# Order of work around the heads of a hybrid decoder layer: twelve key groups ahead of the heads with values in turns, early raw rows, forget sums ahead of a weight split

## The reference

```python
x @ w_in  ->  rq, rk (4 heads x 128, rotary), rv, rg (4 x 256), fq, fk, fv (8 heads x 64), ff, ga, gb (1024 each)
logf = log_sigmoid(ff + b_f)
# prompt: retention in chunks of 128, and forgetting attention:
logits = q k^T / 8 + cumsum(logf)_q - cumsum(logf)_k, causal; p = softmax; o = p v
# samples: retention from a state; attention over 4096 cached rows each, in 32 pages of 128 rows:
k_past = cache_k[page_table]; v_past = cache_v[page_table]; lf_past = cache_logf[page_table]
# merge, then DeepNorm and a causal convolution FFN:
u_a = (silu(rg) * group_norm(ret_o)) @ w_pa;  u_b = fox_o @ w_pb
mix = (sigmoid(ga) * u_a + sigmoid(gb) * u_b) @ w_o
h = layer_norm(2**0.25 * x + mix);  a = gelu(conv(h @ w_up)) * (h @ w_gate)
y = layer_norm(2**0.25 * h + a @ w_down)
```

## Time and profile before

| | |
|---|---|
| median of 3 runs | 2079.36 us (2076.39 to 2080.16) |
| profiled execution | 2078.71 us, of which the span of instructions is 2076.8 us |
| PE busy | 1964.2 us (95%) |
| DVE busy | 1143.8 us (55%) |
| ACT busy | 646.4 us (31%) |
| POOL busy | 195.4 us (9%) |
| mean granted clock of PE | 0.981 |

### The profile page before, as it was taken

How to read it: one execution, slowest core, us unless ns; L and a number is a source line. 1 busy time by engine, 2 the same in 40 slices (tenths; PEclk the granted TensorE clock), 3 DMA queues, 4 the chain that set the end, 5 groups by cost and what they waited for, 6 DMA issues and landing times.

```text
span 2076.8 us, 38216 instructions
## 1 busy us (share of the span) xinstructions
PE 1964.2 (95%) x14259; PEld 1839.1 (89%) x14259; DVE 1143.8 (55%) x1748; ACT 646.4 (31%) x1196; POOL 195.4 (9%) x230
## 2 busy tenths in 40 slices
PE   7999999899999999979899998999999999999996
PEld 5888888788898898868799997999999999999996
DVE  5545646968867866875423857633322333234348
ACT  5445433134134133313401304433202231133334
POOL 1000000111020020010000100000000001000005
PEclk9999999999999999999999999999999999999999
DMA  5111113697987988886833411111111111211154
GB/s 155 43 42 42 41 54 104 216 323 238 323 278 245 314 273 285 285 296 226 283 92 97 119 51 31 32 51 41 51 50 41 51 40 45 58 41 41 38 163 135
DMA packets 151730, 276.63 MB, mean 133 GB/s; under 512 B 19057, under 2 KB 57982, under 8 KB 151590
## 3 DMA queue, kind: packets, MB, share of 16 engines
q1 hardware_dynamic: 115954, 175.22, 25.4%
q0 software_dynamic: 23296, 82.96, 13.7%
q10 hardware_dynamic: 12368, 16.88, 2.2%
HBM read 247.37 MB, written 27.72 MB: 132 GB/s over the span
## 4 chain that ended last, share of the span: by engine, by line
PE 74%; DVE 12%; DMA 4%; issue 4%; SPq 3%; ACT 2%; POOL 0%; ACTq 0%; DVEq 0%; POOLq 0%
PE bank L125 55%; PE bank L142 5%; PE bank L1718 3%; PE bank L521 2%; PE bank L948 2%; DVE cache_keys L1245 2%; PE bank L533 2%; DVE score L1249 2%; SPq L836 2%; DMA cache_keys<-in_cache_k_dram 1%; SPq L828 1%; DMA cache_vals<-in_cache_v_dram 1%; PE banks L505 1%; PE banks L507 1%; DVE w_lo L108 1%
## 5 line engine op out<-in xcount | busy, mean ns | idle before, releaser
L125 PE MATMUL bank<-x_hi,w_hi 128*128 128x344 f32 x1872 | 612.0, 327 | 16.1 <-DVE rot_sin L1315 12.6
L125 PE MATMUL bank<-x_hi,w_lo 128*128 128x344 f32 x1872 | 602.8, 322 | 0.0
L125 PE MATMUL bank<-x_lo,w_hi 128*128 128x344 f32 x1872 | 602.5, 322 | 0.0
L125 PEld LDWEIGHTS bank<-x_hi,w_hi 128*128 128x128 f32 x1872 | 356.3, 190 | 30.0 <-issue 17.4
L125 PEld LDWEIGHTS bank<-x_hi,w_lo 128*128 128x128 f32 x1872 | 356.3, 190 | 0.0
L125 PEld LDWEIGHTS bank<-x_lo,w_hi 128*128 128x128 f32 x1872 | 355.9, 190 | 0.2 <-issue 0.2
L101 ACT ACTIVATE w_hi<-w_raw 128x1024 fp32r<-128x1024 f32 (+3 forms) x139 | 142.1, 1023 | 388.9 <-PE bank L125 371.3
L125 PE MATMUL bank<-moving_lo,w_hi 128*128 128x344 f32 x744 | 239.0, 321 | 0.0
L125 PE MATMUL bank<-moving_hi,w_hi 128*128 128x344 f32 x744 | 226.0, 325 | 9.2 <-DVE moving_lo L1886 3.3
L108 DVE TENSOR_TENSOR w_lo<-w_raw,w_hi 128x1024 fp32r<-128x1024 f32 (+1 forms) x138 | 164.2, 1190 | 87.4 <-ACT w_hi L101 86.8
L125 PE MATMUL bank<-moving_hi,w_lo 128*128 128x344 f32 x648 | 209.0, 323 | 0.0
(11 more groups left out here) (292 smaller groups left out, 2817.8 us busy)
## 6 DMA issues: line engine op xcount, KB each, us to landing
cache_keys<-in_cache_k_dram SPq DMA_DIRECT2D x256, 256.0 KB, 4.9
cache_vals<-in_cache_v_dram SPq DMA_DIRECT2D x256, 256.0 KB, 5.3
w_raw<-in_w_in_dram POOLq DMA_DIRECT2D x52, 512.0 KB, 6.4
w_raw<-in_w_up_dram POOLq DMA_DIRECT2D x22, 512.0 KB, 4.6
w_raw<-in_w_gate_dram POOLq DMA_DIRECT2D x22, 512.0 KB, 4.6
tail_raw<-in_w_down_dram SPq DMA_DIRECT2D x22, 448.0 KB, 3.6
gate<-gate_t_scratch SPq DMA_DIRECT2D x15, 516.0 KB, 3.5
w_raw<-in_w_down_dram POOLq DMA_DIRECT2D x10, 448.0 KB, 4.4
```

Of the source, the lines that this page charges most:

```text
L125: mm = pe.matmul(g.bank[n][0:m, 0:TC], w[slot][:, k, 0:m], x[:, k, chunk(n)], start=(k == 0 and i == 0), stop=(k == kt - 1 and i == 2))
```

## The change

**Start.** The split of the first query weights moves behind the page sums, on ACT behind the copies of the forget logits, on DVE behind the first step of the log sigmoid.

**Heads.** `KEYS_AHEAD` places 12 of sample 0's 16 key groups ahead of the heads, none among the query rotations. The other four, its maximum and shift go into the first head's value products; ACT's exp and GpSimd's maximum move there too, the latter behind the loads of weights 6 and 7. The first head has tables of its own, in which sample 1's keys start at step 4 and sample 0's values at step 6. SP's order follows: one quad of sample 0's values goes between its last two quads of keys, then a quad of sample 1's keys, and so on in turns.

**Raw rows.** Six of the eight gated rows go to a buffer of their own (`gated_early`, over the key slots and part of the bias) and are loaded in pairs right behind the last values, ahead of SP's four small stores. The last two are loaded behind the wait for all stores. ACT waits for the last cache transpose and the stored states at the end of `retain`, DVE for the stored gated rows. `HELD_AFTER` becomes (3, 4, 7).

**Attention tiles.** Two tiles are loaded when the gates' buffers are free, two after the first chunk of the last w_pa product; ACT and DVE split all four in thirds, each third after its chunk of that product.

Moved allocations, counts of semaphores that follow from this, and loops written anew without a change of order are left out below.

```diff
@@ -308,7 +308,6 @@
             round_half(QB, 0, NS, g.xh[:, :, SEQ:T])
-            split_hi(g, act, job(0, 0, 1))
@@ -316,6 +315,7 @@
                 act.activation(rows[s][:, 0:FH], later[s], ACT.Copy).then_inc(first_row, 1)
+            split_hi(g, act, job(0, 0, 1))
@@ -358,7 +358,6 @@
             split_half(QB, 0, NS, slice(SEQ, T))
-            split_lo(g, dve, job(0, 0, 1))
@@ -369,6 +368,7 @@
             ch.link(dve.scalar_tensor_tensor(zn[:], z[:], -1.0, z[:], ALU.mult, ALU.min))
+            split_lo(g, dve, job(0, 0, 1))
@@ -706,6 +706,10 @@
 KEYS_A = (1, 1, 1, 1, 1, 1) + (0, 1, 0, 1, 0, 1, 0, 1, 0) + (1, 0, 1, 0, 1, 0, 1) + (2,)
+KEYS_AHEAD = (0, 0, 2, 1, 2, 1, 0, 1, 5)
+AHEAD = sum(KEYS_AHEAD)
+VALUES_A_FIRST = (0, 0, 0, 0, 0, 0) + (1, 1, 0, 1, 1, 1, 1, 1, 1) + (1, 0, 1, 1, 0, 1, 1) + (1, 0, 1, 1)
+KEYS_A_FIRST = (0, 0, 0, 0, 1, 1) + (1, 0, 1, 1, 0, 1, 1, 0, 1) + (1, 1, 1, 0, 1, 1, 1) + (2,)
@@ -839,45 +844,67 @@
             sp.wait_ge(g.fo_stored, FH // 2 * 16)
...
+            def load_quad(ring, land, used, cache, n, q):
+                ids = page_ids(n, q)
                 for slot in range(SLOTS):
...
+                    load_group(ring, land, used, cache, n, q, slot, ids)
+            def load_both(n, q, of, quad):
+                key_ids, value_ids = page_ids(n, q), page_ids(of, quad)
+                for slot in range(SLOTS):
+                    load_group(keys, k_land, k_used, ck, n, q, slot, key_ids)
+                    load_group(vals, v_land, v_used, cv, of, quad, slot, value_ids)
+            QUADS = NG // SLOTS
+            with sp.Fori(0, QUADS - 2) as q:
+                load_quad(keys, k_land, k_used, ck, 0, q)
+            load_both(0, QUADS - 2, 0, 0)
+            load_quad(keys, k_land, k_used, ck, 0, QUADS - 1)
+            load_quad(keys, k_land, k_used, ck, 1, 0)
+            def period(n, ahead=0):
+                with sp.Fori(ahead, QUADS) as q:
+                    load_both(n + 1, q, n, q)
+            def next_q(n, u):
+                sp.wait_ge(new_mult, n + 1)
+                load_q(n + 2, u)
+            period(0, 1)
+            next_q(0, 0)
+            period(1)
+            next_q(1, 1)
+            with sp.Fori(1, RH - 1) as h:
...
-                    sp.wait_ge(new_mult, h * 2 + u + 1)
-                    load_q(h * 2 + u + 2, u)
+                    next_q(h * 2 + u, u)
             period(NS - 2)
...
+            with sp.Fori(0, QUADS) as q:
+                load_quad(vals, v_land, v_used, cv, NS - 1, q)
+            sp.wait_ge(biased, NS * 2)
+            sp.wait_ge(k_used, NS * NG + SLOTS)
+            sp.wait_ge(g_stored, (RH - 1) * 32)
+            g.load_gated_early(sp)
...
             sp.wait_ge(new_stored, 64)
-            sp.wait_ge(fos_out, NS)
-            for j in range(FH // 2):
-                sp.dma_start(g.fo_dram[j, :, SEQ:T], fos[:, j, :]).then_inc(g.fos_stored, 16)
...
             sp.wait_ge(fin_stored, RH * 16)
+            g.load_gated_late(sp)
+            sp.wait_ge(fos_out, NS)
+            for j in range(FH // 2):
+                sp.dma_start(g.fo_dram[j, :, SEQ:T], fos[:, j, :]).then_inc(g.fos_stored, 16)
@@ -892,7 +919,6 @@
                 load(0, j)
-            all_max(0)
@@ -903,6 +929,8 @@
                     load(h, j)
+                if h == 0:
+                    all_max(0)
@@ -972,7 +1000,7 @@
                 def values_a(e):
-                    for i in take(VALUES_A_LAST if last else VALUES_A, e):
+                    for i in take(VALUES_A_LAST if last else VALUES_A if h else VALUES_A_FIRST, e):
@@ -1135,7 +1163,6 @@
                 gate_chunk(J0 + 3, 3 + n, 0, 1, n, silus[2 + (3 + n) % 4])
-            cache_exp(0, 0)
@@ -1159,6 +1186,8 @@
+                        if h == 0 and w == 5 and n == 1:
+                            cache_exp(0, 0)
@@ -1233,6 +1262,8 @@
             heads(act, body)
+            act.wait_ge(turned, NS)
+            act.wait_ge(fin_stored, RH * 16)
@@ -1325,14 +1356,12 @@
                         split_lo(g, dve, job(J0, 1, 4))
-                    for i in share(NG, 9, 3 * w + n):
+                    for i in take(KEYS_AHEAD, 3 * w + n):
                         cache_logits(0, 0, i)
-            cache_max(0, 0)
-            cache_shift(0, 0)
...
                 def keys_a(e):
-                    for i in take(KEYS_A_LAST if last else KEYS_A, e):
+                    for i in take(KEYS_A_LAST if last else KEYS_A if h else KEYS_A_FIRST, e):
@@ -1347,9 +1376,18 @@
                         keys_a(3 * (w - 4) + n)
-                        if w == 4 and n == 0:
+                        if h and w == 4 and n == 0:
                             cache_sum(h * 2, 0)
+                        if h == 0:
+                            for i in share(NG - AHEAD, 3, n) if w == 4 else ():
+                                cache_logits(0, 0, AHEAD + i)
+                            if w == 4 and n == 2:
+                                cache_max(0, 0)
+                            if w == 5 and n == 1:
+                                cache_shift(0, 0)
                 nxt(6)
+                if h == 0:
+                    cache_sum(0, 0)
@@ -1450,6 +1488,7 @@
             heads(dve, body)
+            dve.wait_ge(g_stored, RH * 32)
@@ -1474,7 +1513,10 @@
     LANDS = 4
-    HELD_AFTER = (2, 5, 7)
+    EARLY_RAW = KD - 2
+    LAND = [(0, 1), (0, 1), (1, 1), (1, 1), (2, 1), (2, 1), (3, 1), (0, 2), (1, 2), (2, 2), (3, 2), (0, 3)]
...
+    HELD_AFTER = (3, 4, 7)
@@ -1501,7 +1543,7 @@
-        fo_slot = [z[:, KB + n, :] for n in range(KB)]
+        g_early = nc.alloc_sbuf_tensor_at("gated_early", [P, EARLY_RAW, T], F32, offset=g.keys_end - EARLY_RAW * T * 4)
@@ -1513,7 +1555,10 @@
-        raw = [g_raw[:, n, :] for n in range(KD)] + [gate[0][:], gate[1][:], stage[0][:, 0:T], fo_slot[3]]
+        raw = [g_early[:, n, :] for n in range(EARLY_RAW)] + [g_raw[:, n, :] for n in range(EARLY_RAW, KD)]
+        fo_raw = [[x[:, chunk(n)] for n in range(NCH)] for x in (gate[1], stage[0])] + [
+            [g_raw[:, at + n, chunk(0)] for n in range(NCH)] for at in (KD - 2 * NCH, KD - NCH)]
@@ -1536,6 +1581,16 @@
+        def load_gated_early(sp):
+            for n in range(0, EARLY_RAW, 2):
+                sp.dma_start(g_early[:, n:n + 2, :], g.g_dram[n:n + 2].rearrange("a p t -> p a t")).then_inc(s_land[LAND[n][0]], 16)
+        def load_gated_late(sp):
+            sp.dma_start(raw[KD - 2], g.g_dram[KD - 2]).then_inc(s_land[LAND[KD - 2][0]], 16)
+            sp.wait_ge(s_hi, 2)
+            sp.dma_start(raw[KD - 1], g.g_dram[KD - 1]).then_inc(s_land[LAND[KD - 1][0]], 16)
...
@@ -1544,25 +1599,21 @@
-                sp.dma_start(raw[n], g.g_dram[n] if n < KD else g.fo_dram[n - KD]).then_inc(s_land[n % LANDS], 16)
...
...
             sp.wait_ge(g.fos_stored, 16 * (FH // 2))
-            for b in (0, 1):
-                for n in range(NCH):
-                    sp.wait_ge(g.bank_free[n], JA + KD - 1 - b + 1)
-                load_raw(KD + b)
-            load_raw(KD + 2)
-            sp.wait_ge(g.mm_chunk, NCH * (RING + JB))
-            load_raw(KD + 3)
-            for i in range(KD, 2 * KD):
-                if i < KD + 2:
-                    sp.wait_ge(s_lo, i + 1)
+            for n in range(NCH):
+                sp.wait_ge(g.bank_free[n], JA + KD - 1)
+            sp.wait_ge(s_hi, KD)
+            sp.dma_start(gate[1][:], g.fo_dram[0]).then_inc(s_land[LAND[KD][0]], 16)
+            sp.dma_start(stage[0][:, 0:T], g.fo_dram[1]).then_inc(s_land[LAND[KD + 1][0]], 16)
+            load_gate(KD)
+            sp.wait_ge(g.mm_chunk, NCH * (RING + JB - 1) + 1)
+            for t, at in ((2, KD - 2 * NCH), (3, KD - NCH)):
+                sp.dma_start(g_raw[:, at:at + NCH, chunk(0)], g.fo_dram[t].rearrange("p (n c) -> p n c", n=NCH)).then_inc(s_land[LAND[KD + t][0]], 16)
+            for i in range(KD + 1, 2 * KD):
+                if i == KD + 1:
+                    sp.wait_ge(s_lo, KD + 2 * KB + 1)
@@ -1638,7 +1689,8 @@
                     product(g, pe, job(it * 2 + JB, JB % 2, u), gh[:, 0:KB, :], gh[:, KB:2 * KB, :], KB,
-                            ready=lambda k: pe.wait_ge(s_lo, KD + k + 1))
+                            ready=lambda k: pe.wait_ge(s_lo, KD + k + 1),
+                            before=lambda n: pe.wait_ge(s_lo, KD + n * KB + KB) if n else None)
@@ -1724,9 +1776,13 @@
         def on_scalar(act):
+            def landed(n):
+                act.wait_ge(s_land[LAND[n][0]], 16 * LAND[n][1])
             def raw_hi(n):
-                act.wait_ge(s_land[n % LANDS], 16 * (n // LANDS + 1))
-                act.activation(gh[:, n % KD, :], raw[n], ACT.Copy).then_inc(s_hi, 1)
+                landed(n)
+                act.activation(gh[:, n, :], raw[n], ACT.Copy).then_inc(s_hi, 1)
@@ -1740,9 +1796,11 @@
             split_hi(g, act, job(JB, JB % 2, 0), KB)
-            act.wait_ge(g.mm_chunk, NCH * (RING + JB))
-            for n in range(KD, KD + KB):
-                raw_hi(n)
```

(15 more changed lines are left out.)

34 lines of the change are left out of this document (8 added, 26 removed).

## The result

The changed kernel takes **0.9907 of the time before, 95% interval 0.9892 to 0.9921**: 19.3 us less (16.4 to 22.5), so 2060.0 us on the scale of 2079.36. Its median over nine runs is 2056.0 (2054.2 to 2066.3), that of the nine of before beside it 2079.1. I had forecast 2046.0 and a range of 2037 to 2059: the direction was right, the gain was 58% of the forecast, and the time lies just above the range. The profiled execution of the changed kernel has a span of 2054.3 us, 22.5 less than before.

What follows compares the result with a forecast made beforehand. TensorE, busy 1964.2 of 2076.8 us, was taken as the bound: only its waits and lower-clock time can be won. Gains 3.2 + 15.4 + 10.3 + 4.5 = 33.4 us, so 2079.36 - 33.4 = 2046.0 us, range 2037 to 2059.

Steps and rivals of the forecast that it cites:

- The raw rows' new wait: At the seam, DVE waits for the last gated rows' store: nothing up to 1 us, us for us beyond.
- head start: Twelve key groups ahead of the heads: 16.8 us lost there, 1.4 left for slips, gain 15.4 us (8 to 16.8).
- start: Start of the program, forget sums before the query weights' split: query product starts earlier, gain 3.2 us (2.7 to 5.5).
- raw rows: Seam with the w_pa products: six of eight rows issued early, 10.3 of 11.2 us lost gained (7 to 11.2).
- thirds: w_pb stretch: attention tiles split in thirds, low halves earlier, 4.5 of 5.4 us lost gained (3.9 to 5.4).
- my sign: Start of the program: the profile after should show the query product from 39.5 to 40.5 us.
- Rival 4: Lower clock comes at waits that stay: 1.6 us a stretch, two of them 3.3, so 2049.3 us; chance 0.06.
- groups 5 to 8 have 2.9 to 4.3 us: Head 0: slack of sample 0's value groups 5 to 8 between landing and PE wanting them, 2.9 to 4.3 us.
- DVE's tightest slacks: Head 0: moved DVE work, w_lo for job 6 and the bank-freeing copy, still in time by 0.4 to 3.3 us.
- rival 2: Seam: ACT's store lands at 1023, not 1019, delaying every low half 4 us: 2050 us; chance 0.08.
- Rival 1: Head 0 gives back more, DVE or a value group late; all 13.3 us come back: 2057 us; chance 0.2.
- Rival 3: Sample 0's values and sample 1's keys lock step over 12 groups: 47 us slower, 2093 us; chance 0.03.

Runs made afterwards that it cites:

- The rows straight from the tile: Changed kernel with page numbers unchecked and low halves in free slots, plus last head's two gated rows split from rv_t, not stored and reloaded: 2037.9 us, ratio 0.9807.

## Why the prediction was wrong, point by point

Two terms failed above all: the 1.4 us that head 0 was to give back (9.2 in the trace), and the prompt heads at zero (4.6). The raw rows' new wait was mis-sized by 2.4.

- **The sum.** Forecast were 33.4 us, the traces show 22.5. The 10.9 us between them are 7.9 of the head start (15.4 to 7.5), 3.4 of the start (3.2 to -0.2 with the prompt heads), 2.4 of the raw rows and 0.3 of the thirds, less 3.1 that the other heads and the rest gave. No part of the change accounts for those 3.1 us; without this luck the time would lie farther from the range.
- **What bounds the kernel** held: every gain and loss is PE idle time or PE time at the lower clock.
- **Start.** The query product started at 38.1, inside the 37.5 to 40.4 that I had worked out though ahead of the 39.5 to 40.5 of my sign, and the 4.4 us are inside 2.7 to 5.5. The step that failed is the one I didn't write: that a gain at the start is a gain at the end. In the trace it was given back, 4.6 us of lower clock over four heads that I had at zero without a reason. Rival 4 named this mechanism, at two places and 3.3 us. Whether the early start itself brought the slow time isn't shown (see above). Alone, the part is worth 2.5 us (0.4 to 4.8).
- **Head start.** The first five products lose nothing, 16.7 us as forecast (head 0's second value product began at 401.1 for 400.9). The step that failed is head 0's slack. I took "1.4 us for what slips"; it gave back 9.2. Two terms were wrong. First, "groups 5 to 8 have 2.9 to 4.3 us": group 4 went out at 418.7 for 415.5 and was still in time, but group 8 landed 4.06 us late. I priced SyncE's loads by landing time and ring slots and left out its own 6 us between rounds, in which it waits for nobody and which the views of waits don't show. Second, DVE's tightest slacks (0.4 to 3.3 us) didn't hold: w_lo and the copy of the values' chunk came 1.2 and 1.3 us late. Between 2 and 6 of the 9.2 us go with the range assertions, that is with SyncE's time between rounds; the rest stays without them. My lower end was 8 us; the trace gives 7.5, and the part alone 7.3 (4.4 to 10.2). One trace of before is a high base here: in eight traces with assertions and without the groups, the first five products and head 0 take 215.2 to 219.8 us, 217.9 on average, and before's 219.8 is the longest; with the groups they take 212.2 and, alone, 211.9. The 3.8 us of the later heads prove nothing: the same eight traces show 446.8 to 453.9 us there.
- **Early raw rows.** 7.9 us of a forecast 10.3, inside 7 to 11.2. The term for DVE's new wait, priced at nothing up to 1 us of delay, was mis-sized: it lasted 6.8 us. This kernel reaches the seam 11.1 us ahead of the one before, so rival 2's store, "at 1023, not 1019", would land at 1011.9; it landed at 1011.6. So rival 2 it is, with 2.4 of its 4 us. The rows straight from the tile confirm it: without that store and the late rows behind it nothing is idle. The store's 7.4 to 9.0 us agree with what the prediction cites from the Trainium skill, page "DMA: Bandwidth & Descriptors", section "Issuing engines are not separate DMA queues": transfers of all engines interleave on the same DMA engines. "No row shows how much" was wrong. The trace of before had the price, in the landing times of its eight stores of gated rows:

```profile
DMA to landing us min/median/max: 2.8/7.0/9.5
```

Only the last two landed after 2.8 and 3.0 us, with no loads of the cache beside them. With the early rows beside them they take what the stores of the other heads take.
- **Thirds.** 4.2 us for 4.5, by the mechanism as told.
- **Rivals and range.** I gave the rivals chances of 0.20, 0.08 and 0.06 one at a time, and let the range end at the worst sum with one slow stretch more (2059.4). Rival 1 came at two thirds of its price (9.2 of 13.3 us given back; all of them would make 2058, not 2057), rival 2 at more than half, and rival 4 at four heads instead of two places. Each shows in the run of its part alone, so none excludes another, and the range should have held at least two of them together. Rival 3, the lock step, didn't come.

## What to carry to other kernels

A sum of gains along one engine is an upper bound: ask of each stage behind a gain whether it can start earlier, with its transfers, its queue and its clock. A stretch with the same short waits can differ by 7 us from one execution to the next through the clock alone, so take several traces before a gain of that size is called lost or won. Price an issuing queue as an engine of its own: what lies between two of its transfers, register loads and assertions too, is a rate, and here it was worth 14 us, three quarters of the whole change. And data that stays on the chip (two rows in a tile) should not make a round trip behind a burst of other transfers.

## What the hardware showed that I had not expected

- Reading eight page numbers with their assertions held SyncE for 2.5 to 2.9 us per list; without the assertions a pair of lists fits in a pause of 2.2 us.
- The four prompt heads do the same work in 300.6 to 307.6 us, by 10.2 to 30.7 us of slow time, and end at 343 to 350 us whether they begin at 37.8 or at 45.0.
- Loading 64 of 128 rows of a page took 4.6 us for 5.2, and slowed the kernel by 9 us.
- Two stores that landed in 2.8 and 3.0 us in the kernel before took 7.4 and 9.0 us behind 3.2 MB of loads that were issued some 5 us ahead of them.
